# First FFN units by row chunk, x and modulation sums on TensorE, x and first weights on ScalarE's queue

## What is computed

```python
mod = silu(c) @ w_ada + b_ada          # 1024 -> 9 x 1024: sh1, sc1, gt1, sh2, ...
u = rms_norm(h, g_ffn1) * (1 + sc1) + sh1
h = h + 0.5 * gt1 * swiglu(u, w_ffn1_in, w_ffn1_out)     # D_FF = 2816
u = rms_norm(h, g_mix) * (1 + sc2) + sh2
h = h + gt2 * hybrid_mixer(u, ...)     # stick-breaking attention and gated delta net
u = rms_norm(h, g_ffn2) * (1 + sc3) + sh3
h = h + 0.5 * gt3 * swiglu(u, w_ffn2_in, w_ffn2_out)
```

## Time and profile before

| | us |
|---|---|
| median of 3 runs | 1373.64 (1373.52 to 1374.59) |
| profiled execution | 1374.76 |
| its span | 1373.0 |
| TensorE busy in it | 1283.7 |
| VectorE, ScalarE, POOL busy | 677.1, 664.9, 84.0 |
| mean granted clock | 0.969 |

### The profile page before, as it was taken

How to read it: one execution, slowest core, us unless ns; L and a number is a source line. 1 busy time by engine, 2 the same in 40 slices (tenths; PEclk the granted TensorE clock), 3 DMA queues, 4 the chain that set the end, 5 groups by cost and what they waited for, 6 DMA issues and landing times.

```text
span 1373.0 us, 16921 instructions
## 1 busy us (share of the span) xinstructions
PE 1283.7 (93%) x6009; PEld 1045.9 (76%) x6009; DVE 677.1 (49%) x937; ACT 664.9 (48%) x1152; POOL 84.0 (6%) x95
## 2 busy tenths in 40 slices
PE   2699999999997999999889979999889999999998
PEld 1588888887775777778668968877668888888887
DVE  6766666664444464665365345465353333332221
ACT  5576666665543696555683432653333223222121
POOL 3000000001110000000203223000200000000000
PEclk8699999999998999999999999999999999999999
DMA  9477676775552232222221020154313333333421
GB/s 324 108 189 188 183 188 183 184 209 150 156 144 62 62 92 77 62 69 77 69 77 47 23 70 24 38 181 127 92 57 97 92 99 99 92 114 102 119 78 31
DMA packets 279951, 152.30 MB, mean 111 GB/s; under 512 B 7877, under 2 KB 275294, under 8 KB 279902
## 3 DMA queue, kind: packets, MB, share of 16 engines
q1 hardware_dynamic: 275678, 149.54, 39.0%
q10 hardware_dynamic: 4224, 2.10, 0.5%
HBM read 145.31 MB, written 6.29 MB: 110 GB/s over the span
## 4 chain that ended last, share of the span: by engine, by line
PE 86%; DVE 5%; ACT 4%; SPq 2%; issue 2%; DMA 1%; ACTq 0%; DVEq 0%
PE region L1227 12%; PE region L1228 12%; PE region L1229 12%; PE tail L1227 12%; PE tail L1228 12%; PE tail L1229 12%; PE region L1531 2%; PE region L1383 2%; PE region L1528 2%; SPq L346 1%; PE region L1518 1%; PE region L1245 1%; PE region L1369 1%; PE region L1418 1%; PE region L1256 1%
## 5 line engine op out<-in xcount | busy, mean ns | idle before, releaser
L481 ACT ACTIVATE w_hi<-raw 128x1024 fp32r<-128x1024 f32 (+1 forms) x181 | 201.7, 1115 | 496.6 <-PE region L1229 242.8
L826 DVE TENSOR_TENSOR w_lo<-raw,w_hi 128x1024 fp32r<-128x1024 f32 (+1 forms) x181 | 235.2, 1300 | 269.0 <-ACT w_hi L481 267.6
L1227 PE MATMUL region<-u_hi,w_hi 128*128 128x512 f32 x672 | 265.7, 395 | 3.7 <-DVE w_lo L826 3.7
L1229 PE MATMUL region<-u_hi,w_lo 128*128 128x512 f32 x672 | 261.7, 389 | 0.0
L1228 PE MATMUL region<-u_lo,w_hi 128*128 128x512 f32 x672 | 261.6, 389 | 0.0
L1227 PEld LDWEIGHTS region<-u_hi,w_hi 128*128 128x128 f32 x672 | 126.1, 188 | 32.8 <-issue 4.7
L1228 PEld LDWEIGHTS region<-u_lo,w_hi 128*128 128x128 f32 x672 | 126.1, 188 | 28.5 <-issue 2.4
L1229 PEld LDWEIGHTS region<-u_hi,w_lo 128*128 128x128 f32 x672 | 126.1, 188 | 26.2
L1227 PE MATMUL tail<-u_hi,w_hi 128*128 128x512 f32 x344 | 144.0, 419 | 1.9 <-DVE w_lo L826 1.9
L1227 PE MATMUL tail<-g_hi,w_hi 128*128 128x512 f32 x352 | 141.1, 401 | 0.0
L1228 PE MATMUL tail<-g_lo,w_hi 128*128 128x512 f32 x352 | 139.0, 395 | 0.0
(11 more groups left out here) (274 smaller groups left out, 1624.2 us busy)
## 6 DMA issues: line engine op xcount, KB each, us to landing
raw<-in_w_ffn_in SPq DMA_DIRECT2D x176, 256.0 KB, 3.4
ada_raw<-in_w_ada SPq DMA_DIRECT2D x56, 512.0 KB, 5.1
raw<-in_w_in SPq DMA_DIRECT2D x90, 256.0 KB, 3.3
raw<-in_w_ffn_out SPq DMA_DIRECT2D x32, 384.0 KB, 4.2
raw<-in_w_ffn_out SPq DMA_DIRECT2D x32, 320.0 KB, 3.5
ada_early<-in_w_ada SPq DMA_DIRECT2D x8, 1024.0 KB, 12.0
kept_gates<-rstd SPq DMA_DIRECT2D x16, 256.0 KB, 3.6
gates<-kept_gates SPq DMA_DIRECT2D x16, 256.0 KB, 3.7
```

Source lines behind the costliest of these rows:

```text
L481: act.activation(w_hi[:, slot % 2, 0:k, :], raw[:, slot, 0:k, :], ACT.Copy).then_inc(hi_ready, 1)
L826: dve.tensor_tensor(w_lo[:, slot % 2, 0:k, :], raw[:, slot, 0:k, :], w_hi[:, slot % 2, 0:k, :].bitcast(f32), ALU.subtract).then_inc(lo_rea ...
L1227: pe.matmul(bank(b), wh, xh, start=start and n == 0, stop=False)
L1229: ins = pe.matmul(bank(b), wl, xh, start=False, stop=stop and n == k - 1)
```

## The change

x and the first four units' weights go through ScalarE's queue, issued before ScalarE's first computation; SyncE asks for c, the small loads and then the 8 pieces, in the order scale columns, shift columns, scale, shift and so on. x is transposed by block of 128 tokens and copied from PSUM by VectorE. The sum of squares is taken over x as it lies in memory (tokens on partitions) by ScalarE with an accumulated output; root and refinement run on 4 columns, and four matmuls spread the result to 128 x 512. A piece is summed by TensorE: 8 f32 matmuls in four column tiles of 32 (`early_piece`), a copy by ScalarE (`early_part`), and two matmuls of one column with `share` (1/32) (`early_totals`). The first four units run with the row chunk outermost: chunk k of all four (12 matmuls) in two halves of 6, with pieces and totals between them; weights are split per chunk (`first_hi`, `first_lo`, 512 columns), and the scale is formed for two chunks at a time (`first_scale`). Unit numbers shift by 4 (`F1_IN`), and the steps of the FFN for j = 0 and 1 follow the block. `refine`, `statistics` and `sum_squares` no longer have a case s = 0, and ScalarE's first lap of the F1_OUT loop is unrolled. "..." marks what is left out.

```diff
 
-F1_IN = 0
+FIRST = 4
...
+def first_tile(k):
+
+    return FIRST * ((k + 2) % 5)
+
+
+def early_col(a):
+
+    return PIECE * (a // 2) + (0 if a % 2 else D)
 
 
...
-                sp.wait_ge(lo_ready, phase + 4 * i + u + 1)
+                if is_static(i) and phase == F1_IN and i == 0:
+                    sp.wait_ge(lo_ready, (2, 5, KD, KD)[u])
+                else:
+                    sp.wait_ge(lo_ready, phase + 4 * i + u + 1)
                 load(phase, i, u + RAW)
...
             sp.dma_start(c_rows[:, :], c[0].rearrange("(k p) -> k p", p=P)).then_inc(c_in, 16)
-            sp.dma_start(ada_early[:, 0], w_ada_v[:, :, 0:PIECE]).then_inc(ada_early_in[0], 16)
-            for b in range(NB):
-                sp.dma_start(x_nat[:, b, :], x[0, b * P:(b + 1) * P, :]).then_inc(x_in, 16)
-            for q in range(1, EARLY):
...
-            for u in range(RAW):
-                load(F1_IN, 0, u)
+            for a in range(EARLY):
+                sp.dma_start(ada_early[:, a], w_ada_v[:, :, early_col(a):early_col(a) + PIECE]).then_inc(ada_early_in[a], 16)
...
-                        split_hi(phase, i, 2 * jj + 2)
-                        act.wait_ge(unit_done, phase + 2 * j + 1)
+                        lead = 2 * jj + 2 if f or not is_static(j) or j > 1 else 4 if j == 0 else None
+                        if lead is not None:
+                            split_hi(phase, i, lead)
+                        if lead == 2 * jj + 2:
+                            act.wait_ge(unit_done, phase + 2 * j + 1)
+                        elif j == 0:
+                            act.wait_ge(unit_done, KD)
+                        else:
+                            act.wait_ge(first_done, 1)
...
+            for b in range(NB):
+                act.dma_start(x_nat[:, b, :], x[0, b * P:(b + 1) * P, :]).then_inc(x_in[b], 16)
+            for k in range(KD):
+                for half in range(2):
+                    act.dma_start(raw_tiles[:, FIRST * k + 2 * half:FIRST * k + 2 * half + 2, :],
+                                  ffn_in_v[0][:, k, half * FF:half * FF + 2 * P].rearrange("p (t n) -> p t n", n=P))\
+                        .then_inc(first_in[k], 16)
+            act.wait_ge(masks, 10)
             act.wait_ge(c_ps, 1)
...
+            act.preload_act_table_set("natural_log_exp_and_others")
+            for b in range(NB):
+                act.wait_ge(x_in[b], 16)
+                if b:
+                    act.wait_ge(tok_sq, b)
+                act.activation(x_sq[:, :], x_nat[:, b, :], ACT.Square, accum_out=tok["sum"][:, b:b + 1]).then_inc(tok_sq, 1)
+            act.wait_ge(tok_sq, NB)
+            act.activation(tok["rstd"], tok["sum"], ACT.Ln, bias=eps[:, 0:1], scale=1.0 / D).then_inc(tok_root, 1)
...
+            act.activation(tok["rstd"], tok["rstd"], ACT.Exp, scale=-0.5).then_inc(tok_root, 1)
+            act.preload_act_table_set("silu_and_others")
...
+            act.wait_ge(tok_ps, 1)
+            act.activation(rstd[:, :], bank(4), ACT.Copy).then_inc(rstd_ready, 1)
+
+            def early_part(a):
+
+                act.wait_ge(early_ps, a + 1)
+                if a >= 2:
+                    act.wait_ge(early_cols, a - 1)
+                act.activation(parts[:, a % 2, :], bank(6 + a % 2)[:, 0:PIECE], ACT.Copy).then_inc(early_copied, 1)
+
+            def first_hi(k):
+
+                act.wait_ge(first_in[k], 32)
+                if k >= 5:
+                    act.wait_ge(unit_done, k - 4)
+                act.activation(wh_tiles[:, first_tile(k):first_tile(k) + FIRST, :],
+                               raw_tiles[:, FIRST * k:FIRST * k + FIRST, :], ACT.Copy).then_inc(hi_ready, 1)
+
+            early_part(0)
+            early_part(1)
             for k in range(KD):
...
-            rough_root(0)
...
+                if k % 2 == 0:
+                    act.wait_ge(early_mod, k + 2)
+                act.wait_ge(normed_ready, k + 1)
+                act.activation(u_hi[:, k, :], work[:, k % 2, :], ACT.Identity,
+                               bias=mod[:, SH[0] * KD + k:SH[0] * KD + k + 1]).then_inc(u_hi_ready, 1)
+                if k % 2 == 0 and k + 2 < KD:
+                    early_part(k + 2)
+                    early_part(k + 3)
             ffn(0, F1_IN)
-            for i in laps(act, KD // 2, 0, 1):
+            for i in laps(act, KD // 2):
...
-                        split_lo(phase, i, 2 * jj + 2)
+                        lead = 2 * jj + 2 if f or not is_static(j) or j > 1 else 4 if j == 0 else None
+                        if lead is not None:
+                            split_lo(phase, i, lead)
...
-            dve.wait_ge(cond_ready, 1)
...
-            for q in range(EARLY):
-                if q in BY_ACT:
-                    n = BY_ACT.index(q)
-                    dve.wait_ge(early_scaled, n + 1)
-                    halve(ada_early[:, q, 0:1, :], ada_early[:, q], early_halves, n)
-                else:
-                    dve.wait_ge(ada_early_in[q], 16)
-                    ada_sum(ada_early[:, q, 0, :], ada_early[:, q], early_step, BY_DVE.index(q))
...
-            split_lo(F1_IN, 0, 0)
-            split_lo(F1_IN, 0, 1)
...
+            for t in range(2 * NB):
+                b, half = t // 2, t % 2
+                dve.wait_ge(x_ps, t + 1)
+                dve.tensor_copy(hT[:, 4 * half:4 * half + 4, b * P:(b + 1) * P], heads(bank(t % 4))).then_inc(h_ready, 1)
...
+            def early_columns(a):
+
+                cols = slice(early_col(a) // P, early_col(a) // P + 2)
+                dve.wait_ge(early_cols, a + 1)
+                dve.tensor_tensor(mod[:, cols], bank(5 - a % 2)[:, cols], vec[:, cols], ALU.add).then_inc(early_mod, 1)
+
+            def first_lo(k):
+
+                dve.wait_ge(hi_ready, k + 1)
+                tiles = slice(first_tile(k), first_tile(k) + FIRST)
+                dve.tensor_tensor(wl_tiles[:, tiles, :], raw_tiles[:, FIRST * k:FIRST * k + FIRST, :],
+                                  wh_tiles[:, tiles, :].bitcast(f32), ALU.subtract).then_inc(lo_ready, 1)
+
+            def first_scale(a):
+
+                early_columns(a)
+                dve.wait_ge(early_mod, a + 1)
+                ks = slice(a, a + 2)
+                ins = dve.scalar_tensor_tensor(scale_col[:, 0, ks], mod[:, KD + a:KD + a + 2], 1.0,
+                                               vec[:, 72 + a:74 + a], ALU.add, ALU.mult)
+                ins.then_inc(early_scale, 1)
+                dve.wait_ge(early_scale, a // 2 + 1)
+
             dve.wait_ge(vec_ready, 2)
-            dve.tensor_tensor(mod[:, 0:LATE], bank(5)[:, 0:LATE], vec[:, 0:LATE], ALU.add).then_inc(early_mod, 1)
-            dve.wait_ge(early_mod, 1)
-            norm(0)
+            first_scale(0)
+            dve.wait_ge(rstd_ready, 1)
+            scaled(0, 0)
+            early_columns(1)
+            scaled(0, 1)
+            for k in range(KD):
+                first_lo(k)
+                low(0, k)
+                if k + 2 < KD:
+                    if k % 2 == 0:
+                        first_scale(k + 2)
+                        early_columns(k + 3)
+                    dve.wait_ge(u_lo_ready, k + 1)
+                    scaled(0, k + 2)
...
+            pe.transpose(bank(6)[:, 0:96], vec_rows[:, :], ident[0:96, 0:96])
+            pe.transpose(bank(6)[:, 128:179], vec2_rows[:, :], ident[0:51, 0:51]).then_inc(vec_ps, 1)
+            pe.wait_ge(tok_ready, 1)
+            for b in range(NB):
+                ins = pe.matmul(bank(4)[:, b * P:(b + 1) * P], tok["rstd"][:, b:b + 1].to_broadcast([P, P]), ident[:, :],
+                                start=True, stop=True)
+            ins.then_inc(tok_ps, 1)
+            pe.wait_ge(cond_ready, 1)
+            pe.wait_ge(vec_ready, 2)
...
+            def early_piece(a):
+
+                pe.wait_ge(ada_early_in[a], 16)
+                if a >= 2:
+                    pe.wait_ge(early_copied, a - 1)
+                for k in range(KD):
+                    t = k % 4
+                    ins = pe.matmul(bank(6 + a % 2)[32 * t:32 * t + 32, 0:PIECE],
+                                    cond[:, k:k + 1].to_broadcast([P, 32]), ada_early[:, a, k, :],
+                                    start=k < 4, stop=k >= 4, tile_position=(0, 32 * t))
+                ins.then_inc(early_ps, 1)
+
+            def early_totals(a):
+
+                pe.wait_ge(early_copied, a + 1)
+                if a == 1:
+                    pe.wait_ge(rstd_ready, 1)
+                if a >= 2:
+                    pe.wait_ge(early_mod, a - 1)
+                for n in range(2):
+                    col = early_col(a) // P + n
+                    ins = pe.matmul(bank(5 - a % 2)[:, col:col + 1], parts[:, a % 2, n * P:(n + 1) * P], share[:, 0:1],
+                                    start=True, stop=True)
+                ins.then_inc(early_cols, 1)
+
+            def first_half(k, j):
+
+                if j == 0:
+                    pe.wait_ge(lo_ready, k + 1)
```

(85 more changed lines are left out.)

133 lines of the change are left out of this document (65 added, 68 removed).

## The result

The changed kernel takes 1383.2 us (median of four runs, 1378.71 to 1384.04) against 1373.67 (1373.52 to 1374.59) for the kernel before: ratio 1.006, 95% interval 1.0044 to 1.0076. On a second chip the pair was 1382.44 (six runs) and 1375.4 (23 runs): ratio 1.0043 (1.0028 to 1.0059). The ratios are not those of the medians; by them the loss is 8.2 and 5.9 us, by the medians 9.5 and 7.0. It is slower. The forecast was +3.5 for the median.

A forecast was written before the change was run, and what follows sets the result against it. TensorE's dense matmul stream was taken to bound the kernel. Unit 6 at 92.2 + 1.7 against 90.28 gave +3.6 us: profiled 1374.76 becomes 1378.4, less 1.1 to the median, 1377.2; range 1368.5 to 1385.

The forecast's parts named there:

- What bounds the kernel: TensorE is 86% of the chain; a change at the start is worth only its effect on when the matmul stream begins.
- Part 1: Prologue until the first matmul of FFN 1: it starts at 27.5, 25 us earlier than 52.38.
- rival 3: Late start: ScalarE's squares, its 20 issues or shared queues delay piece 1 or the root; +4 more, 1381; chance 0.15.
- third term: At the start, shared queues delay piece 1; it decides if that lands beyond 20; priced with both pieces 3 later.
- Part 2: A piece on TensorE: four column tiles side by side take 0.95 us at 2.4 GHz, 1.9 at 1.2 GHz.
- Rival 4: Column tiles of 32 run one after another, each piece 3.4 instead of 0.95: +28, 1402; chance 0.07.
- Part 3: Eight row chunks: TensorE waits about 2.5 in each of three periods; period 11.0 at 2.4 GHz, 18.2 at 1.2 GHz.
- Which clock: TensorE's clock in the first units: +2.0 at the start, 2.2 lost a period, 6.6 in all; unit 3 ends at 74.5.
- Rival 1: The clock stays at 2.4 GHz through the periods of the row chunks: -4.7, 1369; chance 0.20.
- Part 4: Late w_ada pieces before the ada total: TensorE idles 5.3 us, unit 6 starts at 92.2, the clock's fall costs 1.7.
- Rival 2: Late pieces don't hold up unit 6, because loads land sooner than every one in the rows: -3.8, 1370; chance 0.08.
- The sum: At unit 6, 92.2 + 1.7 - 90.28 = +3.6 us: profiled execution 1378.4, predicted median 1377.2.

The follow-up runs named there:

- one-tile kernel: Changed kernel with each piece as eight matmuls on all 128 columns one after another, instead of four column tiles of 32: 1397.88 us, ratio 1.0164.
- Next chunk first: Changed kernel with ScalarE and VectorE splitting and finishing chunk k + 1 before the scale of chunks k + 2 and k + 3: 1369.52 us, ratio 0.996.
- first profile: Profiled execution of the changed kernel on the first chip, shortest of its four: 1378.71 us around a span of 1376.7.
- repeated run: The changed kernel once more with no edit, on a second chip: 1382.44 us, ratio 1.0043; span of the profiled execution 1380.8.

## Why the prediction was right in sign and short in size

**What bounds the kernel.** Right, and the table shows it: an edit at the start is worth what it does to the start of unit 6, to about 2 us.

**Part 1, the start: mis-sized by 3.1.** The forecast had 27.5, the trace 30.57. The step that failed is "20 x 0.38 = 7.6": I took the issue of a 256 KB store at the end of the kernel, with nothing beside it, for loads issued while SyncE issues too. The four of x took 0.46 each (1.85) and the sixteen of the weights 9.43, 0.59 each: 0.47 to 0.87 for the first five, while SyncE issued its small loads, and mostly near 0.49 after that. Whether SyncE, the shape or something else makes them longer than 0.38 no run separates. So all twenty end at 12.1 instead of 8.4, and the silu ends at 13.7 instead of 10.0. A smaller error on top: a square is not 1.06, as I took it, but 1.24 (15.00 to 16.24), since its sum is read by an instruction of 0.19; 0.7 for four. TensorE's broadcasts then ended at 23.3 instead of 18.8; 1.4 came back, because a piece at 1.2 GHz took 1.7 instead of 1.9 and the way from the totals to u_lo was shorter than I had summed. This is rival 3 in part: I gave it as a separate case at +4, and its mechanism (20 issues, squares) was simply what happened. Its third term nearly came true as well: I had piece 0 and 1 landing at 14 and 20, they landed at about 17.7 and 22.6, hidden only because ScalarE was later still. The moved table loads cost what the row of before said: 13.71 to 15.00 is 1.28 and nothing else, so the 2.66 us of the Trainium skill (ScalarE: Activation LUTs, "What ACT_TABLE_LOAD costs") does not show here either.

**Part 2, the piece.** 1.93 for two, 0.97 each, against 0.95 forecast. The one-tile kernel gives the other bound, 3.5 against 3.4. Rival 4 was priced too high: its 28 holds the forecast's own 3.6 and 15 + 10 = 25 for the pieces, and against these 25 stand 16.6 measured. Over half of the difference is the start, where the first matmul is 35.75 - 30.57 = 5.2 later and not 10: the granted clock was 0.99 from 27.0 to 31.9 there, so the second piece did not run at 1.2 GHz as I had taken it.

**Part 3, the chunks.** The period 41.55 to 52.48 is 10.93, forecast 11.0; the holes are 2.34, forecast 2.5, released by the u_lo of the next chunk as forecast. "Next chunk first" shows the cause by removing it.

**Which clock.** The direction held, the size is not one number. I took 2.2 for each of three holes, 6.6. In the first profile only one low stretch of 3.3 us followed (1.6 us lost), in the second three, of 3.2, 3.2 and 6.6 us (the periods 12.53 each instead of 10.93 and the last stretch to unit 4 2.8 longer: 6.0 us lost). Filling the waits gave 5.1 at unit 4 and 6.4 in the median. So 6.6 was near for the repeated run and the medians and too much for the first profile. Rival 1 (the clock stays up) held after two of the three waits in the first profile and after none in the repeated run and in the one with the late pieces moved. That the first profile is the odd one is likely and not shown for each run: it has the highest mean clock of its four, 0.974 against 0.967 to 0.970, and is the shortest.

**Part 4, the late pieces.** The hole is 5.82, forecast 5.3; the chain is the one I described, two slots deep, and moving pieces 0 and 1 takes the hole away. Unit 6 started at 92.63, forecast 92.2 + 1.7 = 93.9. Rival 2 is refuted.

**The sum.** Forecast +3.6, profiled +3.7, and this agreement is partly luck: a start 3.1 too late against a clock that lost 1.6 in the chunks instead of 6.6 (and about 1 more than the 2.0 I gave its first stretch, which lasted to 36.5 and not 4 us), in the shortest of four executions. The step that failed for the median is the last one, from the profiled execution to the median: I moved the forecast by the 1.1 that before's profile lay above its median, as if the changed kernel scattered as before does. Its own profile lies 4.5 below its median. In the repeated run, where the clock did what I forecast, unit 6 is at 95.03 against 89.72, +5.3; the forecast of +3.6 with the 3.1 of Part 1 would be +6.7, and that chip says +7.0 by the medians and +5.9 by the ratio. What the first chip adds to that, 9.5 against 7.0, no run here separates: it can be chip or scatter, with four runs of the changed kernel on one and six on the other.

## What to carry to other kernels

Starting a dense stream earlier is worth only what stays of it after the stream has been broken up: here 22 us of earlier start became 5, and then a loss, through the order of VectorE's instructions and two slots of a buffer, while the same edit with these and the queue of the weights put right gave 20 us. In an order written out by hand, let the operands of what the bounding engine does *next* go before the preparation of what it does after that, and ask of each moved block which slow follower had been hidden beside it. Do not queue DMA issues on an engine that must compute first: they take its time one by one. And look at what lands just before it is wanted: it is the next bound once the first is gone.

## What the runs showed of the hardware

- Issuing a 128 KB load from ScalarE's queue kept that engine for 0.59 us on average (16 in 9.43; single ones 0.45 to 0.87) while SyncE issued too; the 0.38 of the earlier trace rows was for one store alone.
- Four column tiles of 32 run beside each other in f32 at 3.7 times the rate of one tile: 1.93 against 7.07 for two pieces.
- A square with a sum over 1024 columns comes as two instructions, 1.06 and 0.19, and starts every 1.24 us.
- A wait of 2.34 us behind 0.95 us of one-column matmuls lowers TensorE's clock from 2.4 to 1.2 GHz in some executions and not in others. The low stretches cost about 6 us of the median, which came back when matmuls that nobody needs filled the waits: 6.4 by the medians, 5.8 by the ratios, with 2 to 3 us of noise.
